# Two hybrid blocks on one core: attention of block one as a lane beside the delta-rule groups, mixing and output projection by column half

## What is computed

```python
h = rms_norm(x, norm_gain[layer]); proj = h @ w_in[layer]       # 1024 -> 9304 columns
# attention branch: an indexer scores the keys, each query keeps its 64 best causal ones
iscore = einsum(relu(q_i @ k_i), w_i); sel = top_k(iscore, 64)
y_a = softmax(q_a @ k_sel / sqrt(128)) @ v_sel * silu(z_a)      # 8 heads, 2 key/value heads
# delta-rule branch: causal conv of 4 taps, 8 heads, chunked recurrence with an inverse
qkv_b = silu(conv(qkv_b)); o_b = gated_delta_rule(l2(q_b), l2(k_b), v_b, beta, g)
y_b = rms_norm(o_b, gdn_norm_gain) * silu(z_b)
mixed = sigmoid(gate_0) * y_a + sigmoid(gate_1) * y_b
x = x + mixed @ w_out[layer]
```

## Time and profile before

| | us |
|---|---|
| median of 3 runs | 1390.18 (1389.88 to 1391.13) |
| the profiled execution | 1390.79 |
| its span | 1388.9 |
| TensorE matmul busy | 1172.6 |
| VectorE busy | 725.8 |
| ScalarE busy | 574.2 |
| GpSimd busy | 664.4 |

### The profile page before, as it was taken

How to read it: one execution, slowest core, us unless ns; L and a number is a source line. 1 busy time by engine, 2 the same in 40 slices (tenths; PEclk the granted TensorE clock), 3 DMA queues, 4 the chain that set the end, 5 groups by cost and what they waited for, 6 DMA issues and landing times. The chain is left out here.

```text
span 1388.9 us, 17561 instructions
## 1 busy us (share of the span) xinstructions
PE 1172.6 (84%) x6858; PEld 1027.6 (74%) x6858; DVE 725.8 (52%) x1099; ACT 574.2 (41%) x790; POOL 664.4 (48%) x288
## 2 busy tenths in 40 slices
PE   1999979999758699997999974879999677999864
PEld 0999978898547598997889864768788456887743
DVE  2465475653972456447664486244636622653553
ACT  2452236314542356224531453335457342546622
POOL 2664255524334476335642452568436554734643
PEclk9999999999878899999999987889999887999987
DMA  5553243423232355224432331345324415523420
GB/s 184 171 149 92 67 146 111 118 61 106 66 117 70 120 146 146 82 77 122 136 107 61 91 94 59 106 138 157 109 84 128 135 46 182 154 80 95 148 91 31
DMA packets 84433, 152.17 MB, mean 110 GB/s; under 512 B 10560, under 2 KB 16512, under 8 KB 84224
## 3 DMA queue, kind: packets, MB, share of 16 engines
q1 hardware_dynamic: 84352, 151.06, 36.4%
HBM read 149.99 MB, written 1.05 MB: 109 GB/s over the span
## 5 line engine op out<-in xcount | busy, mean ns | idle before, releaser
L739 POOL TENSOR_TENSOR w_lo<-raw,w_hi 128x1024 fp32r<-128x1024 f32 (+3 forms) x284 | 664.2, 2345 | 702.0 <-ACT w_hi L1156 701.7
L1156 ACT ACTIVATE w_hi<-raw 128x1024 fp32r<-128x1024 f32 (+3 forms) x284 | 287.4, 1017 | 566.3 <-PE bulk L791 446.2
L791 PE MATMUL bulk<-w_hi,hT_hi 128*128 128x512 f32 (+1 forms) x800 | 334.3, 418 | 42.9 <-DVE arena L1627 18.0
L791 PE MATMUL bulk<-w_hi,hT_lo 128*128 128x512 f32 (+1 forms) x800 | 321.8, 402 | 0.0
L791 PE MATMUL bulk<-w_lo,hT_hi 128*128 128x512 f32 (+1 forms) x800 | 321.7, 402 | 0.0
L791 PEld LDWEIGHTS bulk<-w_hi,hT_hi 128*128 128x128 f32 x800 | 157.3, 197 | 81.2 <-DVE arena L1627 21.4
L791 PEld LDWEIGHTS bulk<-w_hi,hT_lo 128*128 128x128 f32 x800 | 156.9, 196 | 34.0
L791 PEld LDWEIGHTS bulk<-w_lo,hT_hi 128*128 128x128 f32 x800 | 157.7, 197 | 29.9 <-issue 0.5
L868 PEld LDWEIGHTS chain<-arena 128*128 128x128 f32 x1440 | 170.2, 192 | 7.8 <-DVE arena L1751 2.6
L868 PE MATMUL chain<-arena 128*128 128x128 f32 x1440 | 174.5, 277 | 0.7
L812 PE MATMUL chain<-cst,arena 128*128 128x128 f32 (+2 forms) x512 | 80.4, 306 | 75.6 <-DVE arena L1936 30.6
(11 more groups left out here) (215 smaller groups left out, 1332.5 us busy)
## 6 DMA issues: line engine op xcount, KB each, us to landing
raw<-in_w_in_dram SPq DMA_DIRECT2D x194, 512.0 KB, 3.6
raw<-in_w_out_dram SPq DMA_DIRECT2D x32, 512.0 KB, 3.6
raw<-in_w_branch_dram SPq DMA_DIRECT2D x16, 512.0 KB, 4.0
raw<-in_w_mem_kv_dram SPq DMA_DIRECT2D x8, 512.0 KB, 3.7
raw<-in_w_merge_up_dram SPq DMA_DIRECT2D x16, 256.0 KB, 2.8
raw<-in_w_in_dram SPq DMA_DIRECT2D x8, 420.0 KB, 3.4
gain<-in_ln_rows_dram SPq DMA_DIRECT2D x4, 512.0 KB, 4.6
gain<-in_gains_dram SPq DMA_DIRECT2D x3, 512.0 KB, 4.4
```

The source lines that it names most:

```text
L739: pool.tensor_tensor(lo_of(p, u)[:, 0:n], raw_of(p, u)[:, 0:n], hi_of(p, u)[:, 0:n].bitcast(F32), ALU.subtract).then_inc(p.done("split"), 1)
L791: m = pe.matmul(dst, a, b[:, k, :], start=(kk == 0 and i == 0), stop=(kk == tot - 1 and i == 2))
L1156: return act.activation(dst, src, func, **more)
```

## The change

1. Attention becomes lane b of block one, beside gdn_chain(0) and gdn_chain(1) in lane a. In the new ORDER its indexer part runs between the inverse's first steps of group 0, the top-k inside group 0's inverse and the group's last steps, and the softmax steps among the tiles c11 and c21. To allow it the arena is shared anew (uu over vb, kd and st over xx, sq over yy, qaT over g1, some probabilities over rl and pi), and iT waits no more for o(1,1). qaT over g1 adds the wait of zb's drain for sc(1,1), and za0 is drained before zb0.
2. tap is cut in three steps (tap, tap_on 1, tap_on 2), with no waits between the four instructions of one; topk is cut in four steps for each query block; onorm is done by head group with one tensor_tensor_reduce for each of 16 head and row blocks; norm_c is done by row block.
3. The tiles stand in a new sequence: za0 za1 g00 g01 zb0 zb1 g10 g11 o0 o1. mix_b, mix and mT go by column half h, as a lane x: half 0 needs only g00, g10 and the first four heads. o0 and o1 run their first halves of w_out's rows (o0.0 o0.2 o1.0 o1.2) and then their second; only the second halves wait for mT(1). Block two's o0 and o1 get the same order of units.
4. cwT moves behind the sixth bulk unit, three of the nine parameter loads (those of block two) move behind the first gain load, and the gain load moves behind gc_b, that is behind the loads of units 6 and 7. The transposition of the memory, memT, moves from between the mT steps to behind onorm_c(1).
5. The orders of both layers of block two are written anew, with the same steps.

The core of the diff:

```diff
+ONE_TILES = ones("ba c00 c10 c20 qi ki kv qa0 qa1 c01 c11 c21 za0 za1 g00 g01 zb0 zb1 g10 g11 o0 o1")
 def units_of(tiles):
+    halves = [x for x in out if x[0] in ("o0", "o1")]
+    halves.sort(key=lambda x: x[2] >= KD // 2)
+    return [x for x in out if x[0] not in ("o0", "o1")] + halves
...
 def attention_chain():
-    out = [("iT", r) for r in range(R)]
-    out += [("raw", 0, 0), ("raw", 1, 0), ("raw", 1, 1)] + [("qT", r) for r in range(R)] + [("kaT",)]
-    out += [("topk", 0), ("sc", 0, 0), ("topk", 1), ("pT", 0, 0), ("pv", 0, 0), ("sc", 0, 1), ("onorm_a",), ("onorm",),
-            ("pT", 0, 1), ("pv", 0, 1), ("sc", 1, 0), ("onorm_c",), ("pT", 1, 0), ("pv", 1, 0), ("sc", 1, 1),
-            ("mix_b", 0), ("mix", 0), ("mT", 0), ("mix_b", 1), ("pT", 1, 1), ("pv", 1, 1)]
-    return out + [("mix", 1), ("mT", 1)]
+    out = [("kxT",), ("kinorm_a",), ("kinorm",), ("rope_i",)] + [("iT", r) for r in range(R)]
+    out += [("raw", 0, 0), ("raw", 1, 0), ("raw", 1, 1), ("rope_a",)] + [("qT", r) for r in range(R)] + [("kaT",)]
+    out += [("topk", qb, i) for qb in range(R) for i in range(TOPK // 16)]
+    for kv in range(2):
+        out += [("sc", kv, 0), ("sc", kv, 1), ("pT", kv, 0), ("pv", kv, 0), ("pT", kv, 1), ("pv", kv, 1)]
+    return out
...
 def block_one(l):
-    chain += gdn_chain(0) + [("kxT",), ("kinorm_a",), ("kinorm",), ("rope_i",), ("rope_a",)] + gdn_chain(1)
-    return {"a": [("gain",)] + chain + tail, "b": []}
+    mix = [(step, c) for c in range(2) for step in ("mix_b", "mix", "mT")]
+    return {"a": chain + gdn_chain(0) + gdn_chain(1) + memory, "b": attention_chain(), "x": mix}
...
-    "one": {"ba": [("hT", 1)], "o0": [("mT", 1)]},
+    "one": {"ba": [("hT", 1)], "o0": [("mT", 0)]},
...
-                        for dst, src in loads:
+                        for dst, src in loads[:N_PARAMS]:
...
+                    if w["lhs"] == "mix" and k0 == KD // 2:
+                        pe.wait_ge(*p.after("vector", "mT", 1))
...
+                def tap_one(w, g, k):
+                    b = tile_in(f"c{w}{g}")
+                    back = CONV_K - 1 - k
+                    for j in range(4):
+                        c = k * 24 + w * 8 + g * 4 + j
+                        ins = STT(cv[:, j, back:S], b[:, j * S:(j + 1) * S - back], par1[:, p.l, c:c + 1],
+                                  cv[:, j, back:S], ALU.mult, ALU.add)
+                    return ins
...
-                def mix(r):
-                    v.wait_ge(*p.after("vector", "gmul", "g01"))
-                    v.wait_ge(*p.after("vector", "pv", 1, r))
+                def mix(h):
+                    v.wait_ge(*p.after("vector", "gmul", f"g0{h}"))
+                    for qb in range(R):
+                        v.wait_ge(*p.after("vector", "pv", h, qb))
...
-                def mT(r):
-                    act.wait_ge(*p.after("tensor", "mm", max(u for u, x in enumerate(UNITS["one"]) if x[0] == "g11")))
+                def mT(h):
+                    act.wait_ge(*p.after("tensor", "mm", min(u for u, x in enumerate(UNITS["one"]) if x[0] == "o0") - 1))
```

More of the change, by code:

```diff
@@ L170, in bulk_lanes @@
             if w["src"] == "w_in" and w["col"] >= C_GATE:
-                conv.append(("gmul", name))
-    return {"s": [("split", n) for n in range(len(units))], "m": mm, "c": conv, "d": drains["scalar"], "v": drains["vector"]}
+                gates.append(("gmul", name))
+    return {"s": [("split", n) for n in range(len(units))], "m": mm, "c": conv, "w": gates, "d": drains["scalar"], "v": drains["vector"]}
 def gdn_chain(g):
@@ L181, in gdn_chain @@
             out.append(("invY", g, r, n))
+        if n == len(LEVELS) - 1:
+            out.append(("kT", g))
         for r in range(R):
@@ L186, in gdn_chain, with attention_chain @@
     out += [("kq", g, 0), ("kq", g, 1), ("u", g, 0), ("st", g), ("ks", g), ("o", g, 0), ("u", g, 1), ("o", g, 1)]
[L187 to L199 removed]
+    return out + [("onorm_a", g), ("onorm", g), ("onorm_c", g)]
+def attention_chain():
+    out = [("kxT",), ("kinorm_a",), ("kinorm",), ("rope_i",)] + [("iT", r) for r in range(R)]
[3 more added lines that the diff above has]
+        out += [("sc", kv, 0), ("sc", kv, 1), ("pT", kv, 0), ("pv", kv, 0), ("pT", kv, 1), ("pv", kv, 1)]
+    return out
+NORM = [("norm_a",), ("norm",), ("norm_c", 0), ("norm_c", 1)]
 def block_one(l):
[L204 to L205 removed]
+    chain = [("hT", r) for r in range(R)] + [("baT",), ("ba_a",), ("ba_b",), ("ba_c",), ("gc",), ("gc_b",), ("gain",)]
     if l == 0:
[L207 to L213 removed]
+        chain += [("cwT",), ("tables_a",), ("tables",), ("tables_c",)]
+    mix = [(step, c) for c in range(2) for step in ("mix_b", "mix", "mT")]
+    memory = [("memT", r) for r in range(R)] if l == 0 else []
+    return {"a": chain + gdn_chain(0) + gdn_chain(1) + memory, "b": attention_chain(), "x": mix}
 FOX, MEM, MLA = 2, 3, 0
@@ L991, in pv @@
                     m.then_inc(p.done("pv"), 1)
-                def mT(r):
-                    c = take("mT", r)
-                    pe.wait_ge(*p.after("vector", "mix", r))
-                    transposes(c, [g0[:, r, k * P:(k + 1) * P] for k in range(KD)]).then_inc(p.done("mT"), 1)
+                def mT(h):
+                    c = take("mT", h)
+                    pe.wait_ge(*p.after("vector", "mix", h))
+                    transposes(c, [g0[:, r, k * P:(k + 1) * P] for k in range(4 * h, 4 * h + 4) for r in range(R)]).then_inc(
+                        p.done("mT"), 1)
                 def xT(r):
@@ L1222, in conv_silu @@
                 def conv_silu(w, g):
-                    act.wait_ge(*p.after("vector", "tap", w, g))
+                    act.wait_ge(*p.after("vector", "tap_on", w, g, 2))
                     if (w, g) == (0, 1):
@@ L1547, in norm_a, with norm_c @@
                     TS(nrm[:, 0, :], nrm[:, 2, :], 1.0 / D, EPS, ALU.mult, ALU.add).then_inc(p.done("norm_a"), 1)
-                def norm_c():
-                    v.wait_ge(*p.after("scalar", "norm"))
-                    newton(nrm[:, 1, :], nrm[:, 0, :], nrm[:, 3, :])
-                    v.wait_ge(gain_in, 16 * (p.l + 1) if p.sec == "one" else 16 * (DEPTH + 1))
-                    for r in range(R):
-                        dst = h_nat if p.sec == "one" else xs
-                        ins = STT(dst[:, r, :], xs[:, r, :], nrm[:, 1, r:r + 1], gain[:, :], ALU.mult, ALU.mult)
-                        if r == 0:
-                            ins.then_inc(p.own, 1)
-                            v.wait_ge(*p.last())
-                    ins.then_inc(p.done("norm_c"), 1)
+                def norm_c(r):
+                    if r == 0:
+                        v.wait_ge(*p.after("scalar", "norm"))
+                        newton(nrm[:, 1, :], nrm[:, 0, :], nrm[:, 3, :])
+                        v.wait_ge(gain_in, 16 * (p.l + 1) if p.sec == "one" else 16 * (DEPTH + 1))
+                    dst = h_nat if p.sec == "one" else xs
+                    STT(dst[:, r, :], xs[:, r, :], nrm[:, 1, r:r + 1], gain[:, :], ALU.mult, ALU.mult).then_inc(p.done("norm_c"), 1)
                     v.wait_ge(*p.here("norm_c"))
@@ L2136, in handlers @@
                             memT=memT, tables_a=tables_a, tables_c=tables_c, cwT=cwT, norm_a=norm_a,
-                            norm_c=norm_c, hT=hT, drain_v=drain, gmul=gmul, tap=tap, ba_a=ba_a, ba_c=ba_c, gc=gc_, stat=stat, rn=rn,
+                            norm_c=norm_c, hT=hT, drain_v=drain, gmul=gmul, tap=tap, tap_on=tap_on, ba_a=ba_a, ba_c=ba_c, gc=gc_, stat=stat, rn=rn,
                             dec=dec, dec_c=dec_c, kk=kk, kT=kT, vT=vT, invY=invY, invZ=invZ, kq=kq, ks=ks, o=o_,
```

228 lines of the change are left out of this document (123 added, 105 removed).

## The result

The changed kernel takes 1328.85 us (median of 4 runs, 1327.98 to 1330.21) against 1390.66 for the kernel before (4 runs, 1389.88 to 1391.69): a ratio of 0.956, with a 95% interval of 0.954 to 0.957. The forecast was 1330. The profiled execution took 1328.02, with a span of 1326.2 us; the earlier trace rows has 1388.9.

What follows compares the result with a forecast made beforehand. TensorE bounds the kernel where dense; its 216 us of idle time can be won. Start -17.4, layer step -8.2, tails -28.8 and -29.8, middle +24, block two 0 sum to -60.2: 1330 us, range 1300 to 1360.

Steps and rivals of the forecast that it cites:

- The start: Before layer 0's first unit: with cwT and three loads moved back and an earlier norm, unit 0 starts at 18.3 us, -17.4.
- Layer 0 to 1: Step between the layers: with the gain load behind unit 6, hT's copies no longer wait for a raw load, -8.2 us.
- The tails: End of each block-one layer: 29.8 us idle and 10 or 11 of low clock go, 11 come back: -28.8 and -29.8.
- The middle: Each block-one layer where attention now runs: exposed waits of 20.3 us replace 8.4 at the group change, +12 a layer.
- (d): Middle of each layer: mm(42) waits for tap_on(1,1,2), behind pv(1,1) and two taps on VectorE, 5.0 us.
- (a): Middle of each layer: rope_i, 13.9 us of VectorE, stands ahead of kk(0,1), whose PSUM pair iT(0) needs; 5 us exposed.
- (b): Middle of each layer: raw's hand-overs cost 1.5 us and rope_a ahead of qT 2 (0 to 4).
- (c): Middle of each layer: sc, pT, pv, ks, u and o have hardly a unit between them, 2.4 us exposed.
- (e): Middle of each layer: dec(1,0) waits for rn(1), behind 14.5 us of VectorE work against 10.1 of PE, 4.4 us.
- the first rival: Middle of each layer: rope_i and the taps expose no more than the earlier 8.4 us; 1306 us, 12%.
- The second: Units 24 to 44: GpSimd's splits block VectorE operations with two SBUF inputs, 24 us a layer, half exposed; 1354 us, 20%.
- The fourth: Middle of each layer: attention's 16 hand-overs stay uncovered at 3 us each, 48 a layer; slower, 1414 us, 6%.

## Why the prediction was right, and where it was not

**The start** (-17.4 predicted). Unit 0 starts at 18.30, as worked out: parameters 11.2 us, the norm the rest. For the norm only GpSimd's split was named; the larger part is ScalarE's split, which no longer stands ahead of the norm's root. The step that failed is what stands behind: tables_a on VectorE stands ahead of the taps of tile (0,0), and 5.9 us come back at 53.3. The prediction walked the order only up to unit 0 there. The trace of the changed kernel has a split beside each of three operations of tables_a:

```profile
39.91 2.45 DVE L1520 TENSOR_SCALAR arena<-cst,arena 128x24 f32<-128x24 f32 x1
43.01 2.49 DVE L1534 SCALAR_TENSOR_TENSOR arena<-arena 128x80 f32<-128x80 f32 x1
46.09 2.26 DVE L1541 TENSOR_SCALAR arena<-arena 128x80 f32<-128x80 f32 x1
...
39.93 2.40 POOL L754 TENSOR_TENSOR w_lo<-raw,w_hi 128x1024 fp32r<-128x1024 f32 x1 [1.15 <-ACT w_hi L1176]
43.00 2.41 POOL L754 TENSOR_TENSOR w_lo<-raw,w_hi 128x1024 fp32r<-128x1024 f32 x1 [0.67 <-ACT w_hi L1176]
45.88 2.42 POOL L754 TENSOR_TENSOR w_lo<-raw,w_hi 128x1024 fp32r<-128x1024 f32 x1 [0.47 <-ACT w_hi L1176]
```

Their like beside them takes 0.20 to 0.24, so the three splits cost some 6.5 us, more than the 5.9 that PE waits. By this sum the wait is the splits' work and not the tables' own length; no run took the splits away there.

**Layer 0 to 1** (-8.2). From o1's drain to unit 0 it was 25.8 and is 17.8 us: -8.0. Undone, it costs 7.7 us at its place, and the span of that one execution is 4.7 longer.

**The tails** (29.8 idle, 10 and 11 of clock, 11 back). The idle PE is 6.6 us in layer 0 (340 to 404) and 7.0 in layer 1 (785 to 817) where 11 were predicted. The predicted 2.4 for mT(0)'s low part is 2.55 in the trace. The wait for mT(1) (1.5) is not there. The turn-taking of the two engines was put at 5 us, as PE waiting for splits, and a late mix(0) at 2 with the table load. In the trace they are one wait: PE waits for no split there, but 4.0 and 4.4 us for mix(0), which is late because three operations in front of mT(0) each meet a split. The term of the clock was too large: PE's busy time from unit 0 to unit 0 fell by 5.2 and 5.0 us, not by 10 and 11. The low clock of the tail isn't gone (0.84 in the stretch of the first half), and that behind unit 0 of the next layer is as it was (0.82 over 15.5 us now, 0.81 before, above). Why the term came out at half is open beyond that.

**The middle** (+12 for each layer). Ahead of the tail the idle PE rose by 5.2 us in layer 0, where the wait behind the tables alone is 5.9, and by 3.0 in layer 1. By parts: (d) was right, 4.4 for 5.0. (a) failed in two ways. The order was read as one for both layers, and in layer 0 rope_i stands behind kk(0,1): nothing was exposed there, and 2.3 us in layer 1. And its price was not rope_i's own: the 13.9 us of the earlier trace rows hold five places with operations of 2.2 to 2.6 us, which take 0.2 to 0.5 without a split beside them; in the new places it took 7.0 us in layer 0 (two caught) and 11.8 in layer 1 (four, and one more in kk behind it). (b), raw, exposes nothing in layer 0, and in layer 1 the inverse waits 3.1 us behind it. (c), the softmax's hand-overs, shows no wait of PE over 0.25 us. (e), 4.4 for dec, is not there; a stat of 1.3 is. So block one's middle came nearer to the first rival, the middle that covers itself (no more idle than before), than to the forecast: 8.2 us more of idle PE in both layers, in place of 24.

**Luck in block one.** It is 13.3 us better than forecast, and that is itself a balance: the middle 15.8 us better and the tails' idle PE 9.8, but PE's busy time outside of the steps between layers fell by 8.1 us and not by 21, which is 12.9 worse. With block two's 10.7 us on the other side, it is above all by errors that cancel that the total is right.

**Block two** (0, 6 either way). It cost 10.7 us. Of these 6.3 are idle PE, with waits for the forget gate (3.9 in each layer) and in the softmax of layer 0 that the old order doesn't have. That step failed outright: the prediction said that the products of the merge wait for the same operations in the same order; it is the written order that decides, and it had been rewritten. The other 4.4 are PE's busy time, which the old order doesn't bring back, with the cause open.

**The rivals.** The second was right about the mechanism and too dear in the middle: operations with two SBUF inputs go from 1.23 to 3.3 us beside a split. PE waits for them in the tail (4.0 and 4.4), behind the tables (5.9) and behind rope_i and kk of layer 1 (2.3), and for most of the others not at all. The fourth has no trace. In the prediction's "would show" list, mix's line was to be under 6 us and is 8.5, and the clock of the last 16 units, which was to be near 1, is 0.84 in the 32 us around mT with PE 80% busy.

The Trainium skill (SBUF — State Buffer, "SBUF: two separate sides") has the two engines lock their port pair for a whole instruction, the loser fully blocked. The trace agrees for VectorE (1.23 + 2.4 would be 3.6 at most, 3.3 was measured), and that the split itself goes from 2.4 to 3.1 us fits a wait of GpSimd for VectorE's operation in its turn.

## What to carry to other kernels

When a long softmax tail and a projection that waits for it are both late, move the softmax first: the projection by halves alone, in the one order tried, made the kernel 1% slower, since its tiles' drains and splits stood behind the same queue, and with the tail free it was worth 16 us. In a written order, walk every stage that was rewritten, to the next wait behind the one that went, and price a step from a row without a split beside it, with some 2 us more for each split that it can meet. Of the operations on the chain in front of a stalled PE, take out each one whose inputs are there long before.
